# Two transformer blocks in float32 on one core: the feed-forward layers multiply x before its norm is known

## The reference

```python
h = rmsnorm(x, norm_ffn_g[l])          # x * rsqrt(mean(x*x) + EPS) * g
gt, up = jnp.split(h @ w_ffn_in[l], 2, axis=-1)
x = x + (jax.nn.silu(gt) * up) @ w_ffn_out[l]
```

## Time and profile before

| | us |
|---|---|
| median of 3 runs (1575.06 to 1577.03) | 1576.93 |
| the profiled execution | 1575.61 |
| its span on the core | 1573.8 |
| PE busy | 1524.9 (97%) |
| DVE busy | 1149.3 (73%) |
| ACT busy | 819.0 (52%) |

### The profile page before, as it was taken

How to read it: one execution, slowest core, us unless ns; L and a number is a source line. 1 busy time by engine, 2 the same in 40 slices (tenths; PEclk the granted TensorE clock), 3 DMA queues, 4 the chain that set the end, 5 groups by cost and what they waited for, 6 DMA issues and landing times. The chain is left out here.

```text
span 1573.8 us, 25089 instructions
## 1 busy us (share of the span) xinstructions
PE 1524.9 (97%) x10118; PEld 1342.9 (85%) x10118; DVE 1149.3 (73%) x1497; ACT 819.0 (52%) x1113; POOL 132.6 (8%) x119
## 2 busy tenths in 40 slices
PE   7999999999999999999998899999999999999998
PEld 6999889999799988999987678887888888878887
DVE  6788578786678857878569677777878766776665
ACT  6564453444646445444468654444556565554442
POOL 2060000000115000000004000000111112000000
PEclk9999999999999999999999999999999999999999
DMA  9765466676776646698632247767887765346652
GB/s 328 262 220 201 134 229 221 204 248 231 251 261 215 201 134 231 191 224 278 235 126 95 81 164 277 252 221 208 271 305 237 272 165 197 108 147 215 208 172 102
DMA packets 223762, 327.42 MB, mean 208 GB/s; under 512 B 12216, under 2 KB 175520, under 8 KB 223648
## 3 DMA queue, kind: packets, MB, share of 16 engines
q1 hardware_dynamic: 216584, 315.11, 60.5%
q10 hardware_dynamic: 7064, 10.71, 1.9%
HBM read 316.32 MB, written 9.47 MB: 207 GB/s over the span
## 5 line engine op out<-in xcount | busy, mean ns | idle before, releaser
L1769 DVE TENSOR_TENSOR wparts<-raw,wparts 128x2048 fp32r<-128x2048 f32 (+1 forms) x240 | 545.4, 2278 | 211.3 <-ACT wparts L1286 211.0
L1286 ACT ACTIVATE wparts<-raw 128x2048 fp32r<-128x2048 f32 (+1 forms) x240 | 454.5, 1897 | 117.4 <-PE bank L567 82.7
L565 PE MATMUL bank<-hT,wparts 128*128 128x256 f32 x1216 | 349.4, 287 | 2.7 <-DVE hT L1870 1.5
L566 PE MATMUL bank<-hT,wparts 128*128 128x256 f32 x1216 | 344.7, 283 | 0.0
L567 PE MATMUL bank<-hT,wparts 128*128 128x256 f32 x1216 | 344.7, 283 | 0.0
L565 PEld LDWEIGHTS bank<-hT,wparts 128*128 128x128 f32 x1216 | 233.5, 192 | 7.2 <-issue 5.5
L566 PEld LDWEIGHTS bank<-hT,wparts 128*128 128x128 f32 x1216 | 233.7, 192 | 0.2
L567 PEld LDWEIGHTS bank<-hT,wparts 128*128 128x128 f32 x1216 | 233.6, 192 | 0.0
L565 PE MATMUL bank<-wparts,aT 128*128 128x512 f32 (+1 forms) x536 | 213.9, 399 | 0.5 <-DVE aT L1850 0.5
L566 PE MATMUL bank<-wparts,aT 128*128 128x512 f32 (+1 forms) x536 | 208.6, 389 | 0.0
L567 PE MATMUL bank<-wparts,aT 128*128 128x512 f32 (+1 forms) x536 | 208.4, 389 | 0.0
(11 more groups left out here) (284 smaller groups left out, 1885.0 us busy)
## 6 DMA issues: line engine op xcount, KB each, us to landing
raw<-in_mlp_w SPq DMA_DIRECT2D x64, 1024.0 KB, 5.5
ada_raw<-in_ada_w SPq DMA_DIRECT2D x96, 512.0 KB, 6.6
raw<-in_w_ffn_in SPq DMA_DIRECT2D x44, 1024.0 KB, 5.6
raw<-in_w_in SPq DMA_DIRECT2D x43, 1024.0 KB, 5.8
raw<-in_dil_w_in SPq DMA_DIRECT2D x64, 512.0 KB, 4.9
raw<-in_w_ffn_out SPq DMA_DIRECT2D x22, 1024.0 KB, 5.0
raw<-in_w_o SPq DMA_DIRECT2D x8, 1024.0 KB, 5.1
biasb<-head_bias ACTq DMA_DIRECT2D x16, 512.0 KB, 6.3
```

The source lines that it names most:

```text
L565: pe.matmul(dst, held[:, 0, :], streamed[:, 0, :], start=start, stop=False)
L566: pe.matmul(dst, held[:, 0, :], streamed[:, 1, :], start=False, stop=False)
L1286: act.activation(view(whi[c % SPL], c), view(raw[c % RAW], c), ACT.Copy).then_inc(s_hi, 1)
L1769: dve.tensor_tensor(view(wlo[c % SPL], c), view(raw[c % RAW], c), view(whi[c % SPL], c).bitcast(F32), ALU.subtract).then_inc(s_lo, 1)
```

## The change

1. **Plain x is turned.** PE turns blocks of x itself (`raw_block`): the first four features' blocks before WO3's products, for both halves of the tokens; of the upper four one half right behind WO3, the other inside `first_gate` behind 12 products. ACT and DVE make `hT` from them with the gain alone. `xnf` is gone.
2. **The factor comes later.** `rstd` (per token) is made after all that and spread over the partitions by two products (`spread_rstd`, in the middle of UP 0) and a copy (`rstd_rows`). DVE takes each gate sum out of its bank times `rstd_rows` into `sg`; ACT's Silu runs in place on `sg` and no longer frees the bank. UP's sum stays unscaled; the final sum is multiplied by `rstd` per token as it is added to x.
3. **SP's wait** between UP 0 and GT 1 is on `rstd`, since the scaled x is gone.
4. **Latent heads.** The output chunks MO1 and MO2 are split at step 16 and in `wo` instead of steps 10 and 15, and only four output pieces are left in the heads (steps 15 to 18); chunk 1's four pieces move behind the heads.

```diff
@@ SP, GT/UP chunks
-                    sp.wait_ge(s_xn, 2 * (2 * l + 1) + 2)
+                    sp.wait_ge(s_rstd, RSTD_OF[2 * l + 1] + 2)
@@ latent schedule
-        SPLIT_AT = {0: 4, 3: 5, 6: 6, 10: 7, 15: 8}
-        OUT_PIECES = {12: (0, 0, 0), 13: (0, 0, 2), 14: (0, 1, 0), 15: (0, 1, 2), 16: (1, 0, 0), 17: (1, 0, 2), 18: (1, 1, 0),
-                      19: (1, 1, 2)}
+        SPLIT_AT = {0: 4, 3: 5, 6: 6, 16: 7}
+        OUT_PIECES = {15: (0, 0, 0), 16: (0, 0, 2), 17: (0, 1, 0), 18: (0, 1, 2)}
...
-                for c in (2, 3):
+                for c in (1, 2, 3):
@@ PE
+                    if c == 3:
+                        for t in range(TT):
+                            emptied(pe, ("WO", l, 0, t))
+                        for k in range(DK // 2):
+                            raw_block(k, 0, turned[k])
+                            end(raw_block(k, 1), ("nrm", 2 * l + 1, k))
                     w = weights(("WO", l, c))
                     wide_half(("WO", l, out_half), ("WO", l, c), w, half, None if out_half else ("mg", l))
-                three_for_weights()
-                norm(2 * l + 1, xnf)
+                emptied(pe, ("WO", l, 1, 0))
+                for k in range(DK // 2, DK):
+                    raw_block(k, 0, (sums[0], sums[1], turned[0], turned[1])[k - DK // 2])
...
+                def upper_blocks():
+                    emptied(pe, ("WO", l, 1, 1))
+                    for k in range(DK // 2, DK):
+                        end(raw_block(k, 1), ("nrm", 2 * l + 1, k))
...
+                def spread_rstd():
+                    at = RSTD_OF[2 * l + 1]
+                    pe.wait_ge(s_rstd, at + 2)
@@ ACT
-                for c in range(4):
+                for c in range(3):
                     split_ahead(("WO", l, c))
-                norm_sums(2 * l + 1, sqf)
-                norm_upper(2 * l + 1, xnf)
-                norm_high(2 * l + 1, lambda k: colA[:, c_ffn(l) + k:c_ffn(l) + k + 1])
+                out_square(0, 0)
+                out_square(0, 1)
+                norm_high(2 * l + 1, ffn_gain, range(DK // 2))
+                split_ahead(("WO", l, 3))
+                out_square(1, 0)
+                norm_high(2 * l + 1, ffn_gain, range(DK // 2, DK))
+                out_square(1, 1)
...
                         split_ahead(("GT", l, c))
-                        bk = full(act, ("GT", l, c))
-                        if c >= 2:
-                            emptied(act, ("UP", l, c - 2))
-                        act.activation(sg[c % 2][:, :, :], bk[:, :].rearrange("p (a s) -> p a s", a=2), ACT.Silu)\
-                           .then_inc(drain_sem(("GT", l, c)), 1)
                         split_ahead(("UP", l, c))
+                        emptied(act, ("GT", l, c))
+                        act.activation(sg[c % 2][:, :, :], sg[c % 2][:, :, :], ACT.Silu).then_inc(s_silu, 1)
@@ DVE
+                norm_out(2 * l + 1, ffn_gain, (2, 3))
+                split_ahead(("WO", l, 3))
+                for t in range(TT):
+                    norm_mean(2 * l + 1, t)
...
                         split_ahead(("UP", l, c))
+                        if c == 0:
+                            bk = full(dve, ("rstd", l))
+                            dve.tensor_copy(rstd_rows[:, :], bk[:, 0:S]).then_inc(drain_sem(("rstd", l)), 1)
+                            emptied(dve, ("rstd", l))
+                        bk = full(dve, ("GT", l, c))
+                        dve.tensor_tensor(sg[c % 2][:, :, :], bk[:, :].rearrange("p (a s) -> p a s", a=2),
+                                          rstd_rows[:, :].unsqueeze(1).broadcast_to([P, 2, S]), ALU.mult)\
+                           .then_inc(drain_sem(("GT", l, c)), 1)
                         steps_of(u0 + 3)
-                        emptied(dve, ("GT", l, c))
+                        dve.wait_ge(s_silu, NF1 * l + c + 1)
```

More of the change, by code:

```diff
@@ L637, in choose_slab_banks @@
             def choose_slab_banks():
-                slab_banks[:] = [(n["w"] + i) % WB for i in range(WB)] + [(n["a"] + 4) % AB + WB]
+                slab_banks[:] = [rings["w"][(n["w"] + i) % WB] for i in range(WB)] + [rings["a"][(n["a"] + 4) % AB]]
                 slabs_begun[0] = 0
@@ new lines, in _, with first_gate @@
+                n.update(w=0, a=0)
+                accs = None
+                def upper_blocks():
+                    emptied(pe, ("WO", l, 1, 1))
+                    for k in range(DK // 2, DK):
+                        end(raw_block(k, 1), ("nrm", 2 * l + 1, k))
+                def first_gate(name, w):
+                    bk = begin("w", name)
+                    for ks in (range(DK // 2), range(DK // 2, DK)):
+                        for i in range(2):
+                            for k in ks:
+                                await_pair(("nrm", 2 * l + 1), i, k)
+                                m = mm3(bk[:, S * i:S * i + S], w[:, :, k, P * i:P * i + P], hT[:, :, k, :],
+                                        (i, k) == (0, 0), (i, k) == (1, DK - 1))
+                            if (i, k) == (0, DK // 2 - 1):
+                                upper_blocks()
+                    end(m, name)
@@ L815, in biases @@
+                def spread_rstd():
+                    at = RSTD_OF[2 * l + 1]
+                    pe.wait_ge(s_rstd, at + 2)
+                    bk = begin("a", ("rstd", l))
+                    for t in range(TT):
+                        m = pe.matmul(bk[:, P * t:P * t + P], rstd[:, (at + t) % 2, 0:1].broadcast_to([P, P]), ident[:, :],
+                                      start=True, stop=True)
+                    end(m, ("rstd", l))
                 def biases(*units):
@@ L831, in _ @@
                             w = weights((nm, l, c))
-                            feature_major((nm, l, c), w, (0, P), hT, 0, DK,
-                                          first_of=None if c or i else ("nrm", 2 * l + 1))
+                            if c or i:
+                                feature_major((nm, l, c), w, (0, P), hT, 0, DK, between=idle if c else spread_rstd)
+                            else:
+                                first_gate((nm, l, c), w)
                             used((nm, l, c))
@@ L1335, in h_high, with norm_high @@
                 act.activation(dst, src, ACT.Copy, scale=scale).then_inc(s_hhi, 1)
-            def norm_high(e, gain):
-                for k in range(DK):
+            def norm_high(e, gain, ks=range(DK)):
+                for k in ks:
                     if (e, k) == (0, 2):
@@ L1859, in split_half, with norm_out @@
                                   view(whi[0], 0)[:, rows, :].bitcast(F32), ALU.subtract).then_inc((s_half[2], s_lo)[half], 1)
-            def norm_out(ev, gain):
-                for kp in range(DK // 2):
+            def norm_out(ev, gain, kps=range(DK // 2)):
+                for kp in kps:
                     if (ev, kp) == (0, 1):
@@ L2102, in _ @@
                     half = c - 1
+                    if half:
+                        norm_out(2 * l + 1, ffn_gain, (0, 1))
                     for t in range(TT):
@@ L2176, in _ @@
                     xs = x[:, t, 512 * half:512 * half + 512]
-                    dve.tensor_tensor(xs, xs, bk[:, :], ALU.add).then_inc(drain_sem(nm), 1)
+                    dve.scalar_tensor_tensor(out=xs, in0=bk[:, :], scalar=rstd[:, (RSTD_OF[2 * l + 1] + t) % 2, 0:1], in1=xs,
+                                             op0=ALU.mult, op1=ALU.add).then_inc(drain_sem(nm), 1)
                     if q == 2:
```

37 lines of the change are left out of this document (25 added, 12 removed).

## The result

The changed kernel ran in 1608.22 us (median of five, 1606.3 to 1610.25), the kernel before beside it in 1575.06 (1572.89 to 1577.03): a ratio of 1.0216 with a 95% interval of 1.0204 to 1.0228, slower by 33 us. The profiled execution took 1609.82 with a span of 1608.0; the one of before had 1575.6 and 1573.8.

What follows compares the result with a forecast made beforehand. PE, busy in 97% of the span, was taken as the bound. Factor 27.0, clock 3.4, middle steps 5 and heads -3 sum to 32.4 on the profiled 1575.6: 1608 us, range 1597 to 1617.

Steps and rivals of the forecast that it cites:

- Part 1: At each layer's feed-forward norm: turning x ahead lets GT 0 start earlier, a gain of 2.2 us per layer.
- Part 2: Between UP 0 and UP 1: late rstd delays SP's DMAs and DVE's gate product; 27.0 us for both layers.
- The hidden things: Behind the norm: UP 1's arrival, Silu with possible table load, UP 0's product and DN 0's low part are covered.
- The clock: Behind each layer's long PE gap: a lower granted clock loses 1.7 us, 3.4 together; ends 0 and 5.
- Part 3: Steps 2 to 9 of both layers: PE 0.3 us late at the second bias table, 5 us; between 0 and 10.
- Part 4: Latent heads: moved splits remove a 1.97 us wait and low clock; -3 us, ends 5 won and 3 lost.
- What stood under "would be wrong": At GT 1: wrong if its high part starts before 214, or PE's two long gaps together stay under 25 us.
- SP let go early: Rival at SP's wait: earlier norms meet its rstd count, so GT 1 loads early; 1572 us, chance 0.03.
- The shorter hold-up: Rival at the long gaps: GT 1 lands quicker, clock stays up, DVE just in time for tables; 1598 us, chance 0.13.
- The heads: Rival in the latent heads: pieces behind the heads leave PE waiting, +3 instead of -3; 1614 us, chance 0.12.
- their rival: Rival in the middle steps: each loses 1 us instead of 0.3 as later work is pushed too; 1619 us, chance 0.07.

Runs made afterwards that it cites:

- the kernel that fills the stop: Changed kernel with 108 products, whose result nothing reads, issued by PE behind the step table inside each long gap: 1605.65 us, ratio 1.0197.
- the experiment in the kernel before: Kernel before with only the new latent schedule (splits behind step 16 and behind the heads, four output pieces in the heads): 1572.31 us, ratio 0.9985.
- the kernel with step 0 alone moved: Changed kernel, SP's late wait kept, but in step 0 DVE copies rstd and takes GT 0 from its bank before GT 1's low part: 1598.56 us.
- The version with all products moved: Changed kernel with SP's early release and, in step 0 and every later step, DVE's gate product ahead of the next gate chunk's low part: 1570.12 us, again 1570.07.
- the kernel with the squares first: Changed kernel, but DVE makes the mean squares ahead of UP 0's low part: 1606.42 us, ratio 1.020.

## Why the prediction was right, point by point

The forecast of 1608.0 [1597 to 1617] met 1608.22, by its own mechanism; but its terms were off by up to 3 us each and cancelled, so that the agreement to 0.2 us is luck. On the profiled execution the growth was 34.2 us against 32.4.

- **Part 1 was right.** GT 0's first product follows the first add of x by 13.44 us; forecast was 14.0 (199.7 - 185.7). Blocks are 0.09 us apiece (198.13 - 197.78 for four), not the 0.15 that the earlier trace rows gave, and the wait of 0.5 for the late features did not appear.
- **Part 2 had the right chain, and layer 0 was too dear by 2.9 us.** From the first add of x, GT 1 starts at 41.2 us (225.85 - 184.69) and not at 44.1. Two parts of it were too long. First, rstd stood at 21.1 us (205.81) instead of 22.4: UP 0's low part was done at 19.6 instead of 20.4, and the four small instructions for the mean squares took 0.6 from 204.30 on, not 1.3, while POOL needed 0.9 behind the last of them and not 0.56. Second, the load was quicker. From SP's first small DMA to ACT's copy it is 8.1 us (205.83 to 213.92), not the 9.65 of before, because the load landed in 5.2 us instead of 6.8. In layer 1 it had already been 5.3 before (596.89 to 602.17), and there GT 1's start was met: 42.35 (637.61 - 595.26), with 42.6 forecast (UP 1 at 234.1, less the 5.8 of GT 1 and 185.7). There the stop is 1.2 longer than in layer 0, of which 1.0 is one small DMA issue that took longer (the load leaves 3.86 behind the first one, not 2.86).
- **The hidden things stayed hidden.** ACT's table load, UP 1's arrival and DN 0's low part cost PE nothing there. The stop begins behind the step table and was forecast at 17.1; it is 14.67, and 15.86 in layer 1.
- **The clock was sized too low.** Summed over the windows from the stop on, PE's busy time times what its clock fell short of 1.00 is 2.3 us in layer 0 and 2.9 in layer 1, where 1.7 each stood. PE runs at 0.50, the 1.2 GHz level, for some 4.5 us behind the first stop and 5.7 behind the second. The Trainium skill's rule, in "TensorE: Matmul & The Clock Gate", section "Part 1: The HAM clock gate", that an idle array falls to half rate until work has gone on for a while, is what these rows show, 0.50 in the stop and 0.91 in the window from 230; the kernel that fills the stop shows the other side of it, 1.00 at 226 to 228.
- **Part 3 was right in mechanism, and half again too small:** 7.6 us, not 5. The forecast had PE late by 0.3 us per step; it is 0.38 (the table starts 0.51 behind the product ahead of it instead of 0.13), of which the row prints 0.23 as a wait, and PE's clock is 1.00 all through. Over eight steps that is some 3.1 us a layer, and one longer wait in each layer (0.57 and 1.31) adds 0.3 and 1.1. Moving the product in DVE's order brings all of it back.
- **Part 4: -3.1 against -3**, and 2.9 by the experiment in the kernel before. From the latent norm to the product at 906.67 (870.47 before) both traces take the same 75.9 us, so the gain lies behind it, where the 1.97 us wait and the 1.11 stood.
- **What stood under "would be wrong".** GT 1's high part did start before 214, at 213.92. This execution runs 1.0 us ahead before the change's first instruction: the first add of x, at 185.70 before, is at 184.69 (DVE's rows of before and after):

```profile
185.70 0.68 DVE L2107 TENSOR_TENSOR x<-x,bank 128x512 f32<-128x512 f32 x1
```

```profile
184.69 0.68 DVE L2163 TENSOR_TENSOR x<-x,bank 128x512 f32<-128x512 f32 x1
```

  In the clock of before the part starts at 214.9. The bound stood too close to the forecast of 217.8 for a run-to-run shift, and layer 0's error above used up the rest. The stops, 30.5 us together, kept clear of the 25.
- **Not in the forecast:** 1.8 us between the layers, of which 1.6 is a stretch of lower clock at 502 to 508 behind waits of 1.04 and 0.38 us (the trace of before has 0.91 and 0.39 there, and a clock of 1.00); 1.0 lies behind the latent heads and was not followed up.

The rivals: SP let go early does not happen in this kernel, but forced by hand it gives 1585 and not 1572: `sg` then still stands last on DVE (3.4 us of stop per layer), and the middle takes 143.3 and 146.5 us, 10 more than before and not 5. The shorter hold-up held in part, 2.9 us in layer 0. The heads did not lose, and the middle steps, at 7.6 us, lie nearer to the forecast's 5 than to their rival's 16.

## What to carry to other kernels

When a value's consumer is moved later, look for everything that counts on its semaphore: here a queue that only wanted a place in time waited for rstd, and a line of one wait held 23 of 33 us. The Trainium skill, "Perfetto Trace Analysis", section "Optimization Strategy", says to find the gaps on the engine that should be full and the semaphore behind each, and to make that come sooner; that found the release here, but what DVE's order costs in the middle steps showed fully only once the release was mended. An instruction that frees a bank of the bound engine belongs ahead of weight splits that wait for other engines anyway.

## What was unexpected of the hardware

- A stop of 2.18 us was followed by a clock of 0.50, as the 1.97 of the earlier trace rows had been; stops of 1.18 (at 219.29) were not followed by a lower clock in the windows up to 224. But the length of a stop does not settle it. In the kernel with step 0 alone moved, stops of 2.07 (at 250.91) and 2.10 (656.45) were followed by 1.00 and another of 2.10 (732.73) by 0.52 and 0.63. The version with all products moved has waits of 1.24, 0.32 and 0.36 us at 400 in both of its traces; behind them the clock was 0.68 and 0.50 in the first and 1.00 in the second. So a fall of the clock is no fixed property of a kernel's stop, at these lengths. What decides was not tried.
- 108 products in the stop (13.2 us, 211.05 to 224.26) kept the clock at 1.00; an idle remainder of 1.53 us did not undo it, one of 3.81 in layer 1 was followed by the lower clock.
- A power of 128x1 on POOL took 0.56 us with DVE idle and 2.30 beside DVE's 128x2048 subtraction, and ended 0.4 us behind it, in both layers of the kernel with the squares first. In the trace of before a power of 128x8 took 2.69 at 851.54, begun inside a 128x1024 subtraction (851.37, 1.35 long), where 1.64 is its usual time. That the subtraction holds the power up is a reading of these rows; it was not tried by itself.
- The same load in the same place took 6.8 us from issue to ACT's copy in layer 0 before, 5.2 after, and 5.3, 5.4 and 7.5 in layer 1 of before, after and the filled stop. A chain that hangs on one load is no better known than this, some 2 us; what sets it was not tried.
